# A two-layer transformer trunk on one core: the last gate stage with tokens on partitions, a reordered attention step, and other first microseconds

## What is computed

```python
for i in range(DEPTH):
    x = x + 0.5 * swiglu(rmsnorm(x, ln_ffn1[i]), w_ffn1_gu[i], w_ffn1_down[i])
    h = rmsnorm(x, ln_mix[i])
    x = x + (even_mixer(h, ...) if i % 2 == 0 else odd_mixer(h, ...))
    x = x + 0.5 * swiglu(rmsnorm(x, ln_ffn2[i]), w_ffn2_gu[i], w_ffn2_down[i])
    gate = jax.nn.sigmoid(rmsnorm(x, ln_ple[i]) @ w_ple_gate[i])
    x = x + gate * (p[i] @ w_ple_proj[i])
return rmsnorm(x, ln_final)
```

## Time and profile before

| | us |
|---|---|
| median of 3 runs | 1084.52 |
| lowest and highest | 1080.85, 1088.51 |
| the profiled execution's own time | 1088.08 |
| its span, first to last instruction | 1086.4 |
| PE busy | 1058.0 |
| DVE busy | 764.1 |
| ACT busy | 594.2 |
| POOL busy | 67.9 |

### The profile page before, as it was taken

One profiled execution on the slowest core, in us unless ns is written; L12 is line 12 of the kernel. 1 busy time (PEld: TensorE's weight loads), 2 busy tenths in 40 slices (PEclk: granted clock), 3 DMA queues, 4 the chain that ended last, 5 costly groups with the idle time before them and its releaser, 6 DMA issues. The chain is left out here.

```text
span 1086.4 us, 18558 instructions
## 1 busy us (share of the span) xinstructions
PE 1058.0 (97%) x6712; PEld 940.2 (87%) x6712; DVE 764.1 (70%) x1354; ACT 594.2 (55%) x1030; POOL 67.9 (6%) x100
## 2 busy tenths in 40 slices
PE   7999999999989999999999999999998999999996
PEld 6888888999878888888888888889987888888886
DVE  5978766666546978765688877665767697776665
ACT  6556545435546656544565656445666665654553
POOL 1000001000002000001020000010103200000101
PEclk8999999999999999999999999999999999999998
DMA  9665457663322765447646564468633276545731
GB/s 294 215 200 185 141 150 212 188 201 117 116 79 88 252 195 171 141 143 213 201 155 210 179 195 141 142 178 271 219 99 115 88 233 198 188 138 151 216 117 39
DMA packets 225863, 183.94 MB, mean 169 GB/s; under 512 B 4664, under 2 KB 224528, under 8 KB 225808
## 3 DMA queue, kind: packets, MB, share of 16 engines
q1 hardware_dynamic: 222576, 181.42, 53.2%
q10 hardware_dynamic: 3232, 1.80, 0.6%
HBM read 182.02 MB, written 1.06 MB: 169 GB/s over the span
## 5 line engine op out<-in xcount | busy, mean ns | idle before, releaser
L766 DVE TENSOR_TENSOR wsp<-raw,wsp 128x1024 fp32r<-128x1024 f32 (+1 forms) x382 | 418.2, 1111 | 68.8 <-ACT wsp L510 62.0
L1098 PE MATMUL ps<-xsA,wsp 128*128 128x512 f32 x1056 | 372.9, 398 | 6.2 <-DVE wsp L766 4.8
L510 ACT ACTIVATE wsp<-raw 128x1024 fp32r<-128x1024 f32 (+1 forms) x382 | 355.9, 958 | 22.9 <-PE ps L1091 20.4
L1099 PE MATMUL ps<-xsA,wsp 128*128 128x256 f32 x1056 | 296.1, 280 | 0.0
L1098 PEld LDWEIGHTS ps<-xsA,wsp 128*128 128x128 f32 x1056 | 199.4, 189 | 54.6 <-issue 6.6
L1098 PE MATMUL ps<-hff,wsp 128*128 128x512 f32 x704 | 246.6, 395 | 0.0
L1099 PEld LDWEIGHTS ps<-xsA,wsp 128*128 128x128 f32 x1056 | 200.4, 190 | 0.0
L1099 PE MATMUL ps<-hff,wsp 128*128 128x256 f32 x704 | 196.9, 280 | 0.0
L1098 PEld LDWEIGHTS ps<-hff,wsp 128*128 128x128 f32 x704 | 132.1, 188 | 31.5
L1099 PEld LDWEIGHTS ps<-hff,wsp 128*128 128x128 f32 x704 | 132.8, 189 | 0.0
L1098 PE MATMUL ps<-xsB,wsp 128*128 128x512 f32 x352 | 126.5, 403 | 2.3 <-DVE xsB L830 2.1
(11 more groups left out here) (181 smaller groups left out, 1280.9 us busy)
## 6 DMA issues: line engine op xcount, KB each, us to landing
raw<-in_w_ffn_gu_dram SPq DMA_DIRECT2D x87, 1024.0 KB, 5.1
raw<-in_w_ffn_down_dram SPq DMA_DIRECT2D x64, 704.0 KB, 4.6
raw<-in_w_in_even_dram SPq DMA_DIRECT2D x12, 1024.0 KB, 5.4
raw<-in_w_in_odd_dram SPq DMA_DIRECT2D x9, 1024.0 KB, 6.0
raw<-in_w_ple_gate_dram SPq DMA_DIRECT2D x8, 1024.0 KB, 6.0
raw<-in_w_out_even_dram SPq DMA_DIRECT2D x4, 1024.0 KB, 5.1
raw<-in_w_out_odd_dram SPq DMA_DIRECT2D x4, 1024.0 KB, 5.6
raw<-in_w_ple_proj_dram SPq DMA_DIRECT2D x2, 1024.0 KB, 5.3
```

The lines of the kernel that those rows point to most:

```text
L510: act.activation(wsp[:, s, 0, half * n:(half + 1) * n], raw[:, s, half * n:(half + 1) * n], ACT.Copy).then_inc(hi, 1)
L766: dve.tensor_tensor(wsp[:, s, 1, sl], raw[:, s, sl], wsp[:, s, 0, sl].bitcast(F32), ALU.subtract).then_inc(lo, 1)
L1098: pe.matmul(ps[:, bank, :], whi, moving.rearrange("p s t -> p (s t)"), start=first, stop=False)
L1099: return pe.matmul(ps[:, bank, SEQ:], wlo, moving[:, 0, :], start=False, stop=last)
```

## The change

- **Last layer's gated embedding** (`ple_rows`): the activations are now the fixed operand and the weights stream, so tokens come out on partitions. The projection is 4 tiles of 512 columns, then 16 transposes bring `xT` to tokens on partitions, then 8 gate tiles: four quarters of the width for tokens 0 to 127, the same four for tokens 128 to 255. ACT's sigmoid takes the row's factor as its scale, ACT sums the squares of each quarter by its accumulator, DVE takes the last root per half of the tokens, and the store is halved between queues (ACT's stores the low 512 columns, SP's the high). The final gain comes as rows by a DMA.
- **Mixers**: heads are taken in pairs by DVE and ACT; `values_pair` comes first in its step; `middle` goes ahead of the tile, but for odd steps of softmax heads. The sliding-window bias is one table times a slope inside L977's successor (no more POOL scaling), and the sink is a column of `probs` that the exponential's accumulator adds in.
- **Roots**: `inverse_root` works on each of two columns apart, without a wait between the two. At norm 0 it comes before the third chunk's split.
- **Start**: 16 more warming products after the transposes; units are split between the first blocks; the first tile waits for half chunks.
- **Seam into the second layer** (norm 4): both tiles of the first chunk do their first six `k`, then the last two of each; `spread_rows` is in the middle of the fourth tile.
- **First layer's gated embedding**: DVE's units for projection tiles 1 and 3 now come behind `inverse_root`.

```diff
+PROJ_ROWS = [(t, half) for t in range(TOK) for half in range(2)]
+GATE_ROWS = [(t, r) for t in range(TOK) for r in range(4)]
+ROW_BANKS = (6, 0, 1)
+X_BANK = 2
...
+pool.wait_ge(f_step, 1)
 for h in range(HEADS):
     g = 3 * HEADS + h
-    if h >= 2:
-        pool.wait_ge(logits_ready, 2 * (soft_no[g - 2] + 1))
-    pool.tensor_scalar(bias_swa[:, h % 2], dist_swa[:], 2.0 ** -(h + 1), None, ALU.mult).then_inc(swa_bias, 1)
-for norm in range(6, 9):
+    pool.wait_ge(exp_done, 2 * (soft_no[g - 2] + 1))
+    pool.tensor_copy(probs[:, g % 2, P:LOGITS + 2:2 * P + 1], nsink[:, h:h + 1].broadcast_to([P, TOK])).then_inc(sink_set, 1)
+for norm in range(6, 8):
...
 act.wait_ge(gains_ready, 1)
 for b in range(4):
-    if b == 2:
-        advance(2)
     act.wait_ge(x_turned, b + 1)
     for m in (2 * b, 2 * b + 1):
         act.activation(xsA[:, m, 0, :], ps[:, 2 + b, (m % 2) * SEQ:(m % 2 + 1) * SEQ], ACT.Copy,
                        scale=gain(0, m)).then_inc(xs_hi, 1)
+    advance(min(b + 1, 2))
 advance(4)
 first_copies(0)
...
+def weights_of(g):
+    s, b, swa = g % 2, soft_no[g], g >= 3 * HEADS
+    if swa:
+        act.wait_ge(sink_set, g - 3 * HEADS + 1)
+    for t in range(TOK):
+        act.wait_ge(logits_ready, 2 * b + t + 1)
+        row = probs[:, s, prob_cols(t, swa)]
+        act.activation(row, row, ACT.Exp, bias=negmax[:, s, t:t + 1], scale=-1.0,
+                       accum_out=rowsum[:, g % 4, t:t + 1]).then_inc(exp_done, 1)
...
+if i < n and is_sb[g]:
+    k = stick_no[g]
+    row = probs[:, g % 2, 0:LOGITS]
+    act.wait_ge(sb_abs, k + 1)
+    act.activation(row, row, ACT.Exp, scale=-1.0).then_inc(sb_e, 1)
+    act.wait_ge(sb_e, k + 1)
+    act.activation(row, row, ACT.Ln, bias=1.0).then_inc(sb_log, 1)
+elif i < n and i % 2 == 0:
+    weights_of(g)
+    weights_of(g + 1)
...
+def ple_rows(ph_proj):
+    advance(2 * (ph_proj.c0 + 2))
+    nc.scalar.preload_act_table_set("sigmoid_and_others")
+    done = KD * ph_proj.layer
+    for i, (t, half) in enumerate(PROJ_ROWS):
+        next_tile()
+        act.activation(proj[:, 4 * t + 2 * half:4 * t + 2 * half + 2, :],
+                       ps[:, ROW_BANKS[i % 3], :].rearrange("p (r n) -> p r n", r=2), ACT.Copy).then_inc(proj_ready, 2)
+        advance(ptr[0] + (0, 1, 1, 0)[i])
+    def squared(i):
+        t, r = GATE_ROWS[i]
+        act.wait_ge(row_sum, i + 1)
+        if i >= 2:
+            act.wait_ge(row_squared, i - 1)
+        act.activation(sq[:, i % 2], yT[:, i], ACT.Square, accum_out=row_sq[:, i:i + 1]).then_inc(row_squared, 1)
+    def scaled(t):
+        act.wait_ge(rfin_ready, t + 1)
+        act.wait_ge(row_scaled, 4 * t + 2)
+        act.activation(yN[:, t, 0:D_MODEL // 2], yN[:, t, 0:D_MODEL // 2], ACT.Copy, scale=rfin[:, t:t + 1]).then_inc(y_low, 1)
+        act.wait_ge(y_low, t + 1)
+        act.dma_start(out[0, t * P:(t + 1) * P, 0:D_MODEL // 2], yN[:, t, 0:D_MODEL // 2]).then_inc(stored, 16)
+    act.wait_ge(rcol_ready, 8)
+    for i, (t, r) in enumerate(GATE_ROWS):
+        next_tile()
+        if i >= 2:
+            act.wait_ge(row_sum, i - 1)
+        act.activation(gate_n[:, i % 2], ps[:, ROW_BANKS[(i + 1) % 3], 0:SEQ], ACT.Sigmoid, scale=rcol[:, t:t + 1]).then_inc(row_gate, 1)
+        if i:
+            squared(i - 1)
+        advance(ptr[0] + 2)
+        if i == 5:
+            scaled(0)
+    squared(len(GATE_ROWS) - 1)
+    scaled(1)
...
+dve.tensor_scalar(nhalf[:], var[:], -0.5, None, ALU.mult).then_inc(nstep, 1)
+state["n"] += 1
 step(dve.tensor_scalar(rcol[:].bitcast(I32), var[:].bitcast(I32), 1, None, ALU.logical_shift_right))
 step(dve.tensor_scalar(rcol[:].bitcast(I32), rcol[:].bitcast(I32), -1.0, float(MAGIC), ALU.mult, ALU.add))
-step(dve.tensor_scalar(nhalf[:], var[:], -0.5, None, ALU.mult))
-for _ in range(2):
-    step(dve.tensor_tensor(rtmp[:], rcol[:], rcol[:], ALU.mult))
-    step(dve.tensor_tensor(rtmp[:], rtmp[:], nhalf[:], ALU.mult))
-    step(dve.scalar_tensor_tensor(rcol[:], rtmp[:], 1.5, rcol[:], ALU.add, ALU.mult))
-step(dve.tensor_tensor(rtmp[:], rcol[:], rcol[:], ALU.mult))
-step(dve.tensor_tensor(rtmp[:], rtmp[:], nhalf[:], ALU.mult))
-last = dve.scalar_tensor_tensor(rcol[:], rtmp[:], 1.5, rcol[:], ALU.add, ALU.mult)
+def square_term(t):
+    y = rcol[:, t:t + 1]
+    return dve.tensor_scalar(rtmp[:, t:t + 1], y, y, nhalf[:, t:t + 1], ALU.mult, ALU.mult)
+def corrected(t):
+    y = rcol[:, t:t + 1]
+    return dve.tensor_scalar(y, rtmp[:, t:t + 1], 1.5, y, ALU.add, ALU.mult)
+for turn in range(3):
+    square_term(0)
+    step(square_term(1))
+    corrected(0)
+    last = corrected(1)
+    if turn < 2:
+        step(last)
 last.then_inc(rcol_ready, 1)
 dve.wait_ge(rcol_ready, norm + 1)
-if norm == 8:
+if norm == 7:
...
 dve.tensor_copy(gains[:, DEPTH * KD:], ps[:, 7, DEPTH * KD:(4 * DEPTH + 1) * KD]).then_inc(gains_ready, 1)
 advance(4)
+inverse_root(0)
+dve.wait_ge(in_rel, 16)
+dve.tensor_copy(rel_sb[:, 257:], rel_sb[:, 256:257].broadcast_to([HEADS, 3 * P - 257])).then_inc(rel_ext, 1)
+advance(6)
...
+elif i < n and i % 2 == 0:
+    logits(g)
+    logits(g + 1)
+    advance(units)
+    normalise(g)
+elif i < n:
+    normalise(g)
+    advance(units)
+else:
+    advance(units)
+if 3 <= i and i % 2 == 1:
...
-if (kind, m) != ("g", KD - 1):
+if kind == "p" and m < 5:
+    due += PLE_UNITS[kind][m]
+elif (kind, m) != ("g", KD - 1):
     advance(ptr[0] + due)
...
+def ple_rows(ph_proj):
+    advance(2 * (ph_proj.c0 + 2))
+    inverse_root(7)
+    advance(2 * (ph_proj.c0 + 3))
+    dve.wait_ge(in_gain, 16)
+    dve.wait_ge(x_natural, 1)
+    done = KD * ph_proj.layer
+    def step(ins):
+        state["n"] += 1
+        ins.then_inc(nstep, 1)
+        dve.wait_ge(nstep, state["n"])
+    def final_root(t):
+        v, y, tmp, half = var[:, t:t + 1], rfin[:, t:t + 1], rtmp[:, t:t + 1], nhalf[:, t:t + 1]
+        sums = [row_sq[:, 4 * t + r:4 * t + r + 1] for r in range(4)]
+        dve.wait_ge(row_squared, 4 * t + 3)
+        step(dve.tensor_scalar(tmp, sums[0], sums[1], sums[2], ALU.add, ALU.add))
+        step(dve.tensor_scalar(tmp, tmp, D_MODEL * EPS, None, ALU.add))
+        dve.wait_ge(row_squared, 4 * t + 4)
+        step(dve.tensor_scalar(v, sums[3], tmp, 1.0 / D_MODEL, ALU.add, ALU.mult))
+        dve.tensor_scalar(half, v, -0.5, None, ALU.mult).then_inc(nstep, 1)
+        state["n"] += 1
+        step(dve.tensor_scalar(y.bitcast(I32), v.bitcast(I32), 1, None, ALU.logical_shift_right))
+        step(dve.tensor_scalar(y.bitcast(I32), y.bitcast(I32), -1.0, float(MAGIC), ALU.mult, ALU.add))
+        for turn in range(3):
+            step(dve.tensor_scalar(tmp, y, y, half, ALU.mult, ALU.mult))
+            last = dve.tensor_scalar(y, tmp, 1.5, y, ALU.add, ALU.mult)
+            if turn < 2:
+                step(last)
+        last.then_inc(rfin_ready, 1)
+        dve.wait_ge(rfin_ready, t + 1)
+    def scaled(t):
+        Q = 3 * SEQ
+        dve.tensor_scalar(yN[:, t, 2 * SEQ:Q], yN[:, t, 2 * SEQ:Q], rfin[:, t:t + 1], None, ALU.mult)
+        dve.scalar_tensor_tensor(yN[:, t, Q:], yT[:, 4 * t + 3, :], rfin[:, t:t + 1], gain_rows[:, Q:],
+                                 ALU.mult, ALU.mult).then_inc(y_high, 1)
+    for i, (t, r) in enumerate(GATE_ROWS):
+        cols = slice(r * SEQ, (r + 1) * SEQ)
+        g = gate_n[:, i % 2]
+        dve.wait_ge(proj_ready, done + 4 * t + r + 1)
+        dve.wait_ge(row_gate, i + 1)
+        dve.tensor_tensor(g, g, proj[:, 4 * t + r, :], ALU.mult).then_inc(row_prod, 1)
+        dve.wait_ge(row_prod, i + 1)
+        x_nat = ps[:, X_BANK + 2 * t + r // 2, (r % 2) * SEQ:(r % 2 + 1) * SEQ]
+        dve.tensor_tensor(yT[:, i, :], x_nat, g, ALU.add).then_inc(row_sum, 1)
+        if r < 3:
+            dve.wait_ge(row_sum, i + 1)
+            dve.tensor_tensor(yN[:, t, cols], yT[:, i, :], gain_rows[:, cols], ALU.mult).then_inc(row_scaled, 1)
+        else:
+            dve.wait_ge(row_sum, i + 1)
+        advance(ptr[0] + 2)
+        if i == 4:
+            final_root(0)
+            dve.wait_ge(row_scaled, 4)
+            scaled(0)
+    final_root(1)
+    dve.wait_ge(row_scaled, 6)
+    scaled(1)
...
+if norm == 4:
+    chunk_ready(c0)
+    for ks in (range(KD - 2), range(KD - 2, KD)):
+        for n in range(2):
+            if ks[0] == 0:
+                reuse(n)
+            for k in ks:
+                ready = (xs_lo, KD * norm + k + 1) if n == 0 else None
+                mm = wide_product(n, chunk_w(c0 % RING, k, n * P), xs[:, k], k == 0, k == KD - 1, ready)
+            if k == KD - 1:
+                mm.then_inc(tile_done, 1)
+    column_sums(norm)
+for r in range(norm == 4, 2):
+    if norm or r:
+        chunk_ready(c0 + r)
     for n in range(2):
         bank = 2 * r + n
         reuse(bank)
         tile8(bank, (c0 + r) % RING, n * P, xs, KD * norm if (r, n) == (0, 0) else None, xs_lo,
-              form=wide_product)
+              form=wide_product, halves=c0 if norm == 0 and (r, n) == (0, 0) else None,
```

(46 more changed lines are left out.)

207 lines of the change are left out of this document (88 added, 119 removed).

## The result

The changed kernel took 1077.02 us (median of 20 runs, 1069.77 to 1082.49), the kernel before, on the same chip, 1088.1 (median of 20, 1080.85 to 1091.84). The ratio is 0.9911, with a 95% interval of 0.9893 to 0.9929: faster by 0.9%, 7.7 to 11.6 us. The profiled execution took 1079.73 with a span of 1078.0, against 1088.08 and 1086.4, 8.4 less. The forecast had 1072.7 on the median of three runs, by a gain of 11.8.

The account below looks back on a forecast made before the run. TensorE (PE) was taken to bound the kernel, mostly by steady weight products, so only idle time, half clock and the ends could be won. Gains of 2.2 + 1.9 + 4.2 + 0.5 + 3.0 = 11.8 us gave 1072.7, range 1064 to 1080.

Parts of the forecast that it names:

- within 1%: Outcome class for the whole kernel: time within 1% of the kernel before; chance 0.47.
- faster by over 1%: Outcome class for the whole kernel: time below 1073.7 us; chance 0.47.
- Start, 2.2: Kernel start: clock held by warming, third chunk split behind the root, its products at 25.9 against 28.12; gain 2.2 us.
- Stick steps, 1.9: First mixer: `middle` ahead of the tile removes 3.1 us of waits, 1.2 left between stages; gain 1.9 us.
- rival of waits that only move: Both mixers: waits move instead of going, mixers give 1 us instead of 6.1, time 1077.8; chance 0.15.
- Odd mixer, 4.2: Odd mixer: `osp` wait 2.00, half clock 1.7 and row waits 1.2 go, 0.7 comes back; gain 4.2 us.
- First gate stage and seam, 0.5: First gate stage to second layer: root wait of 1.3 goes, deferred units delay the last blocks; gain 0.5 us.
- the case in which the clock falls: Seam: half clock behind a 2.4 us wait, ending at 575.7 (-0.2 us) instead of 574.0 (+1.5).
- Last gate stage and end, 3.0: Last layer's gates to the end: last product 1.8 us later, then a 7.8 us chain; gain 3.0 us.
- the clock isn't held: Start and seam: clock falls, both win nothing, total gain 9.1 us, time 1075.4; chance 0.18.
- More than the sum: Whole kernel: all upper bounds but the end are reached, gain 19 us, time 1065.5; chance 0.11.
- slower: Mixers: `middle` late by 0.8 us in some 30 steps, kernel 18 us slower, 1103; chance 0.06.

Follow-up runs that it names:

- e3_no_second_warming: Changed kernel with 0 in place of the 16 second warming matmuls; third chunk's first product 7.44 us behind the second split, against 7.42.
- e11_whole_first_chunk: Changed kernel without second warming, first tile waiting for the whole first chunk; third chunk's first product 9.02 us behind the second split, against 7.42.
- e7_root_of_single_steps: Changed kernel with the old root of 13 waited steps on both columns; root 2.57 us, third chunk's product 0.64 earlier, seam 46.70 against 46.77.
- e10_units_before_root: Changed kernel with the first gate stage's two units split before the root again; gates and seam stretch 46.76 us against 46.77.

## Why the prediction came out as it did

**The sum was right, within 0.2 us** (11.8 against 11.7 by the stretches). In part that is luck: the seam gave 1.0 more than I had, the last gate stage and end 0.8 less, the first mixer 0.3 less, and they cancel. Of my classes "within 1%" came, to which I had given the same chance as to "faster by over 1%"; the forecast's own band, 1069 to 1077, was missed by 0.02 us. The time, 1072.7, was 4.3 below the median, and nearly all of that is not in the change. The three runs shown had a median of 1084.52 where 20 runs gave 1088.1; that is 3.6, about one draw of the pitch. The levels can be checked: the spans less their high draws are 1086.4 - 6.6 = 1079.8 and 1078.0 - 9.9 = 1068.1, and with 1.7 around them 1081.5 and 1069.8. The lowest of 20 runs were 1080.85 and 1069.77; with four high draws it would be 13.2 more, and the highest were 1091.84 and 1082.49. Twenty runs of either therefore spread over 11 to 13 us, and the measured ratio carries that.

**Start, 2.2: measured 2.27, by half another reason.** VectorE's chain is what I said: two tiles before 18.57, the root at 3.25 (3.1), the split behind it. But my reason for the clock, the 16 warming products, isn't needed: it holds without them, where the first tile begins on half a chunk behind 2.5 us of idle (`e3_no_second_warming`), and falls behind 4.45 with neither (`e11_whole_first_chunk`). That my number came out is luck as far as the halves brought it: I had given them no term. The Trainium skill (VectorE: DVE Perf Modes, Rules for kernel authors) says to minimise the number of chained operations, not their semaphores; `e7_root_of_single_steps` agrees, 13 waited steps took 2.57 and the 16 operations, in part unwaited, 3.25.

**Stick steps, 1.9: measured 1.61.** One `probsT` wait of 0.67 is left between the stages, as forecast. With two for `probs`, 0.35 and 0.71, the waits left are 1.73 where I had 1.2. The rival of waits that only move fell.

**Odd mixer, 4.2: measured 4.07.** The sum held; of its parts, 1.4 remain as waits (0.68 of issue at the values, 0.67 for `probsT`), where I had 0.7. With that my own terms make 3.5, and where the other 0.5 comes from no run shows. My text left open which engine's order removes the wait for `osp`; when asked, I named TensorE's, and that was wrong.

**First gate stage and seam, 0.5: measured 1.52.** I chose the case in which the clock falls. It fell in 2 of the 10 profiles that have the wait of 1.8 and no longer one behind it, and in all three with one of 2.08 or 2.09. Had I taken the held clock, the forecast's own line gave 1.5. That the deferred units make VectorE late by as much as the root's wait was is what `e10_units_before_root` showed. But the wait is not the one that I described, 2.4 us behind twelve `k`:

```profile
556.92 0.40 PE L1235 MATMUL ps<-xsB,wsp 128*128 128x512 f32 x1
...
560.66 0.50 PE L1235 MATMUL ps<-xsB,wsp 128*128 128x512 f32 x1 [1.80 <-DVE xsB L887]
```

```profile
560.13 0.47 DVE L887 SCALAR_TENSOR_TENSOR xsB<-xT,gains,xsB 128x256 fp32r<-128x256 f32 x1
```

It is 1.80 us behind five `k`, for the sixth block. I had looked at the last two blocks alone, and VectorE's 3.08 a gate tile makes the sixth late already. Behind it seven more `k` fill the time to the last two blocks, ready at 563.3 and 563.7, not at 564.2 and 564.7.

**Last gate stage and end, 3.0: measured 2.2.** Up to the last product it is right within 0.1 (the two waits are 0.4 less than I had, the rest as much more). The term that was too small is the chain behind it, 8.5 and not 7.8: root 2.35 (1071.62 to 1073.97) for 2.1, and 3.3 from the store's issue to the end for 2.8. The 2.3 for a landing came from stores that the earlier trace rows had already spread over 2.01.

The rival *the clock isn't held* did not come at the start, and at the seam it was a matter of chance. *More than the sum* and *slower* did not come.

## What to carry to other kernels

Before a change of under 1% is judged by two profiles, compare a stretch in which both do the same: here any of four such stretches can differ by 3.3 us, by a draw, and only the rest of the span tells of the change. A wait is worth what the stretch around it gets shorter: 1.3 us of a wait removed by deferring work came back in full at the next hand-over, while an order that puts six pairs of the next tile in front of the last two blocks is worth 2.0. And a row of small products that looks like waste may be the cover of a chain on other engines: see who waits for that chain before taking it apart.
